# A two-block transformer kernel: normed rows transposed in token halves, routing done on both halves at once, one semaphore raised earlier

## What is computed

```python
# first block
xn = rms_norm(h, g_mix)                       # "xn" in the kernel
merged = sigmoid(gate_conv) * conv_o + sigmoid(gate_attn) * attn_o
h = h + merged @ w_out                        # the units "ax{t}{n}"
h = h + hierarchical_moe(rms_norm(h, g_ffn))  # "rn"; 4 groups of 8 experts, top 2 of one group
x = rms_norm(h, g_final)                      # "fn"
# second block
z  = modulate(rmsnorm(x), sh1, sc1)           # "zn"
hc = modulate(rmsnorm(ctx), csh1, csc1)       # "cx", gives keys and values of the context
x = x + g1 * mix(z, kv of hc)                 # ends in merged @ w_out, the units "bx{t}{n}"
x = x + g2 * peer(modulate(rmsnorm(x), sh2, sc2))   # "pn"; top 16 keys, rows fetched from tables
return rmsnorm(x, final_norm_g)
```

## Time and profile before

| what | value |
|---|---|
| median of 3 runs | 1789.43 us (1788.4 to 1790.45) |
| profiled execution, device time | 1789.33 us |
| its span on the core | 1787.5 us |
| PE busy | 1488.1 us (83%) |
| DVE busy | 856.4 us (48%) |
| ACT busy | 319.9 us (18%) |
| mean granted clock of PE | 0.914 |

### The profile page before, as it was taken

The page is one execution under the profiler, slowest core; times in us unless marked ns, Lnnn a source line. Parts: engine busy times, 40 slices in busy tenths (PEclk is TensorE's granted clock), DMA queues, the critical chain, the costliest instruction groups (busy, mean ns, idle before and its releaser), DMA issues.

```text
span 1787.5 us, 17480 instructions
## 1 busy us (share of the span) xinstructions
PE 1488.1 (83%) x6161; PEld 835.2 (47%) x6161; DVE 856.4 (48%) x1957; ACT 319.9 (18%) x632; POOL 491.9 (28%) x526
## 2 busy tenths in 40 slices
PE   6989896999999999979889999339486675849497
PEld 5866555344444434337558859314232232314143
DVE  3787125132323232235561129793847657584804
ACT  3123212110101111120330011303121111212110
POOL 1000000000000000000000004577777776777673
PEclk9999996999999999989999999769797888879699
DMA  9629572799999999974201355899999999999995
GB/s 301 249 95 336 204 274 81 318 426 428 429 428 429 428 429 428 428 275 142 94 1 59 118 212 201 307 409 409 409 409 409 409 409 409 409 410 408 406 410 214
DMA packets 135034, 565.36 MB, mean 316 GB/s; under 512 B 11350, under 2 KB 17463, under 8 KB 122493
## 3 DMA queue, kind: packets, MB, share of 16 engines
q1 hardware_dynamic: 60996, 295.88, 41.5%
q0 software_dynamic: 73968, 268.70, 38.1%
q10 hardware_dynamic: 8, 0.01, 0.0%
HBM read 563.49 MB, written 1.06 MB: 316 GB/s over the span
## 4 chain that ended last, share of the span: by engine, by line
PE 75%; DMA 10%; DVE 6%; POOL 4%; issue 3%; ACT 1%; SPq 0%; ACTq 0%; DVEq 0%; POOLq 0%
PE psum L375 52%; PE psum L952 21%; DMA ring<-in_peer_v_dram,attnT 5%; POOL ring L1113 4%; DMA ring<-in_peer_u_dram,attnT 2%; DVE scratch L2019 2%; DMA ring<-in_ada_w_dram 2%; DVE arena L1508 1%; DMA ring<-in_w_in_dram 0%; PE psum L730 0%; PE psum L736 0%; ACT actT L1150 0%; PE psum L805 0%; DVE ring L1878 0%; DVE ring L1880 0%
## 5 line engine op out<-in xcount | busy, mean ns | idle before, releaser
L952 PE MATMUL psum<-ring,arena 128*128 128x512 f32 x960 | 428.1, 609 | 215.3 <-DMA ring<-in_peer_v_dram,attnT 215.3
L1113 POOL DMA_INDIRECT ring<-in_peer_u_dram,attnT x256 | 240.2, 938 | 1189.4 <-DVE attnT L1993 1083.7
L952 PEld LDWEIGHTS psum<-ring,arena 128*128 128x128 f32 x960 | 187.4, 196 | 455.4 <-issue 321.6
L2019 DVE CUSTOM_DVE_ANT_0 scratch<-ring,psum 128x1024 f32<-128x1024 f32 x256 | 309.4, 1220 | 175.3 <-DMA ring<-in_peer_u_dram,attnT 165.2
L375 PE MATMUL psum<-ring,arena 128*64 128x512 f32 (+1 forms) x1552 | 345.2, 596 | 8.4 <-DVEq L1775 8.4
L375 PE MATMUL psum<-actT,ring 128*128 128x256 f32 (+1 forms) x1424 | 262.6, 346 | 7.0 <-DMA ring<-in_w_in_dram 4.6
L1113 POOL DMA_INDIRECT ring<-in_peer_v_dram,attnT x256 | 245.8, 960 | 79.4 <-issue 67.1
L375 PEld LDWEIGHTS psum<-actT,ring 128*128 128x128 f32 x1424 | 234.1, 194 | 34.1 <-issue 10.0
L375 PEld LDWEIGHTS psum<-ring,arena 128*64 128x64 f32 (+1 forms) x1552 | 110.7, 138 | 227.4 <-issue 205.4
L1402 ACT ACTIVATE arena<-ident,attnT 128x128 f32<-128x128 f32 x240 | 87.1, 396 | 218.6 <-PE psum L952 218.0
L1783 DVE TENSOR_TENSOR arena<-arena,psum 128x512 f32<-128x512 f32 x16 | 16.9, 1057 | 214.4 <-PE psum L375 214.4
(11 more groups left out here) (345 smaller groups left out, 1161.7 us busy)
## 6 DMA issues: line engine op xcount, KB each, us to landing
ring<-in_w_up_dram SPq DMA_DIRECT2D x32, 2048.0 KB, 15.7
ring<-in_w_down_dram SPq DMA_DIRECT2D x32, 2048.0 KB, 13.9
ring<-in_w_gate_dram SPq DMA_DIRECT2D x32, 2048.0 KB, 11.9
ring<-in_w_in_dram SPq DMA_DIRECT2D x15, 2048.0 KB, 12.9
ring<-in_ada_w_dram SPq DMA_DIRECT2D x12, 2048.0 KB, 11.5
ring<-in_w_out_dram SPq DMA_DIRECT2D x4, 2048.0 KB, 8.4
ring<-in_peer_wq_dram SPq DMA_DIRECT2D x4, 2048.0 KB, 10.5
ring<-in_w_attn_out_dram SPq DMA_DIRECT2D x2, 2048.0 KB, 8.7
```

Source lines behind the costliest of these rows:

```text
L952: last = nc.tensor.matmul(psum[:, 4 + 2 * t + n, :], diag[:, i, :], row_buf(b)[:, n * 512:(n + 1) * 512], start=first, stop=final)
L1113: pool.indirect_dma_start(out=row_buf(b), out_offset=None, in_=tab, in_offset=bass.IndirectOffsetOnAxis(ap=rowid[:, j // 4, k:k + 1], axis ...
L2019: V.tensor_tensor_reduce(dotjunk[:, i % 2, :], row_buf(b), x, 1.0, 0.0, ALU.mult, ALU.add, dots[:, t, k:k + 1]).then_inc(ev("dotted"), 1)
```

## The change

It does five things.

1. xn, rn and zn are transposed by token halves, as pn was (`half_T`, `half_out`): two banks for each half, the first emptied by ACT, the second by DVE. `tokens_T` and `pn_out` become these helpers. For xn, DVE empties its banks ahead of the rest of its parameter copies.
2. The transposes of the first half of rn and of pn stand on PE between the third and the fourth unit of the output projection. DVE norms half 0 of rn ahead of the fourth addition, and the routing matmuls of half 0 need only half 0 of `actT`.
3. The routing operations on DVE work on both halves at once where they can; the largest values and their places, which can't, are paired. The two negations (`rt_ng`, `rt_nv`) move behind `rows_out(1)`, and ACT empties `ckv0` and `ckv1` ahead of the exponentials that need them.
4. `mixed` is raised ahead of `rows_out(1)`.
5. ACT computes one square root of a constant ahead of the norm fn, after the expert loop.

```diff
+            def half_T(name, rows, ev_name, t):
+                pe.wait_ge(ev(ev_name), t + 1)
+                for n in range(2):
+                    b = bank(f"{name}{t}{n}")
+                    for c in range(4):
+                        last = nc.tensor.transpose(psum[:, b, c * P:(c + 1) * P], rows[:, t, (4 * n + c) * P:(4 * n + c + 1) * P], ident[:, :])
+                    last.then_inc(bank_full[b], 1)
...
-            out_proj(place1, "a")
-            to_T("rn", scratch, "rn_ready")
-            for g in range(4):
-                emptied(pe, f"rn{g}")
-            b = bank("route")
-            for t in range(NT):
+            pe.wait_ge(ev("amerged"), 1)
+            for t, n in ((0, 0), (0, 1), (1, 0)):
+                out_unit_rows(place1, "a", t, n)
+            half_T("rn", scratch, "rn_ready", 0)
+            out_unit_rows(place1, "a", 1, 1)
+            def route(t, b):
+                halves_out("rn", t)
...
+            half_T("rn", scratch, "rn_ready", 1)
+            b = bank("route")
+            route(0, b)
+            route(1, b).then_inc(bank_full[b], 1)
...
-            to_T("zn", scratch, "zn_ready")
-            for g in range(4):
-                emptied(pe, f"zn{g}")
+            for t in range(NT):
+                half_T("zn", scratch, "zn_ready", t)
             landed(place2, "q")
             w = pview(place2, "q")
             for t in range(NT):
+                halves_out("zn", t)
...
-            out_proj(place2, "b")
+            pe.wait_ge(ev("bmerged"), 1)
+            for t, n in ((0, 0), (0, 1), (1, 0)):
+                out_unit_rows(place2, "b", t, n)
+            half_T("pn", scratch, "pn_ready", 0)
+            out_unit_rows(place2, "b", 1, 1)
             everyday.append((4, 5, 6, 7))
...
+            a(nc.scalar.activation(stat("warm", 1), epscol[:, 0:1], ACT.Sqrt))
             squares("fn", resid, "moe_added", normjunk)
             squares("zn", resid, "x2_ready", normjunk)
-            take_T("zn", modsc[:, 0, :], mod[:, 0:KD, 0])
+            for t in range(NT):
+                half_out("zn", t, modsc[:, 0, :], mod[:, 0:KD, 0])
...
+            add_in(0, 0)
+            add_in(0, 1)
+            v(V.tensor_copy(stat("dummy", 1), epscol[:, 0:1]), "ah_ready")
+            rn_rows(0)
+            add_in(1, 0)
+            half_out("rn", 0, xgain)
+            add_in(1, 1)
+            v(V.tensor_copy(stat("dummy", 1), epscol[:, 0:1]), "ah_ready")
+            rn_rows(1)
+            half_out("rn", 1, xgain)
...
+            dve.sem_inc(ev("mixed"), 4)
             rows_out(1)
+            for t in range(NT):
+                v(V.tensor_scalar(stat("rt_ng")[:, t:t + 1], gm[:, 8 * t:8 * t + 1], -1.0, None, ALU.mult), "rt_gmax" if t else None)
+            for t in range(NT):
+                v(V.tensor_scalar(stat("rt_nv")[:, t:t + 1], em[:, 8 * t:8 * t + 1], -1.0, None, ALU.mult), "rt_top" if t else None)
             pair_rows(slotrel, 2)
...
             n_iter = dve.value_load(trips[0:1, 0:1], min_val=STEPS, max_val=MAXSTEPS)
-            dve.sem_inc(ev("mixed"), 4)
             dve.wait_ge(ev("pairx_ready"), 4)
```

More of the change, by code:

```diff
@@ L639, in merge, with out_unit_rows @@
                             last.then_inc(bank_full[b], 1)
-            def out_proj(pl, tag):
-                pe.wait_ge(ev(f"{tag}merged"), 1)
-                for t in range(NT):
[L644 to L650, removed]
+            def out_unit_rows(pl, tag, t, n):
+                landed(pl, f"wo{n}")
+                w = pview(pl, f"wo{n}")
+                b = bank(f"{tag}x{t}{n}")
+                for k in range(KD):
+                    last = mm(psum[:, b, :], mergedT[:, k, t * P:(t + 1) * P], w[:, k, :], k, KD)
+                last.then_inc(bank_full[b], 1)
             attend1()
@@ L872, in _ @@
                 last.then_inc(bank_full[b], 1)
-            out_proj(place2, "b")
-            everyday.append((4, 5, 6, 7))
[L877 to L884, removed]
+            pe.wait_ge(ev("bmerged"), 1)
[3 more added lines that the diff above has]
+            out_unit_rows(place2, "b", 1, 1)
+            everyday.append((4, 5, 6, 7))
             def tokens_back(t):
-                for n in range(2):
-                    emptied(pe, f"pn{t}{n}")
+                halves_out("pn", t)
                 for n in range(2):
@@ L914, in key_scores @@
                 last.then_inc(bank_full[b], 1)
-            tokens_T(0)
-            for n in range(2):
-                emptied(pe, f"pn0{n}")
+            halves_out("pn", 0)
             queries(0, 0)
-            tokens_T(1)
+            half_T("pn", scratch, "pn_ready", 1)
             for g in range(4):
@@ L1151, in take_T, with half_out @@
                     last(ins, f"{name}{g}")
+            def half_out(name, t, scale, bias=None):
+                ps = full(act, f"{name}{t}0")
+                for c in range(4):
+                    kw = {} if bias is None else {"bias": bias[:, c:c + 1]}
+                    ins = nc.scalar.activation(actT[:, c, t * P:(t + 1) * P], ps[:, c * P:(c + 1) * P], ACT.Identity, scale=scale[:, c:c + 1], **kw)
+                last(ins, f"{name}{t}0")
             def copy_out(name, dst, w=512, func=ACT.Copy, **kw):
@@ L1254, in _, with square @@
             squares("cx", ctxr, None, qjunk)
-            squares("rn", resid, "ah_ready")
-            take_T("rn", xgain)
+            def square(tag, src, ready, t, junk=scratch):
+                act.wait_ge(ev(ready), t + 1)
+                a(nc.scalar.activation(junk[:, t, :], src[:, t, :], ACT.Square, accum_out=stat(f"{tag}_ss")[:, t:t + 1]))
+                a(nc.scalar.activation(stat(f"{tag}_sd")[:, t:t + 1], stat(f"{tag}_ss")[:, t:t + 1], ACT.Sqrt, bias=epscol[:, 0:1], scale=1.0 / D), f"{tag}_sd")
+            square("rn", resid, "ah_ready", 0)
+            half_out("rn", 0, xgain)
+            square("rn", resid, "ah_ready", 1)
+            half_out("rn", 1, xgain)
             take_T("cx", modsc[:, 1, :], mod[:, 0:KD, 1])
+            for t in range(NT):
+                ps = full(act, f"ckv{t}")
+                nc.scalar.activation(kvt[:, t * T:t * T + P], ps[:, 0:P], ACT.Copy)
+                last(nc.scalar.activation(vtok[:, 2 + t, :], ps[:, P:2 * P], ACT.Copy), f"ckv{t}")
             act.wait_ge(ev("rt_gmax"), 1)
@@ L1341, in _ @@
                 copy_out(f"keyT{g}", keysT[:, 4 * g:4 * g + 4, :].rearrange("p c n -> p (c n)"))
-            def pn_out(t):
-                ps = full(act, f"pn{t}0")
-                for c in range(4):
-                    ins = nc.scalar.activation(actT[:, c, t * P:(t + 1) * P], ps[:, c * P:(c + 1) * P], ACT.Identity,
-                                               scale=modsc[:, 2, c:c + 1], bias=mod[:, 24 + c, 0:1])
-                last(ins, f"pn{t}0")
             def pn_square(t):
```

113 lines of the change are left out of this document (59 added, 54 removed).

## The result

The changed kernel takes 1767.97 us in the median of 4 runs (1767.25 to 1769.0), the kernel before 1789.94 us beside it. The ratio is 0.9877, interval 0.9865 to 0.9889: 22.0 us gained, where 17.2 were forecast. The time lies in the forecast range, near its lower end, so a part of the gain was not in the sum. The profiled execution takes 1767.25 us, its span 1765.4 (1787.5 before). PE is busy for 1485.8 us, 2.3 less than before, its mean granted clock is 0.919. What went is mostly waiting.

The account below looks back on a forecast made before the run. PE was taken to bound the expert loop, so gains come only where PE idles or runs slowly. 0 + 9.1 + 4.3 + 3.8 = 17.2 us off 1789.3, plus 0.1 for the median, gives 1772.2 us; range 1767.5 to 1777.5.

Parts of the forecast that it names:

- xn: At the start: evictions finish sooner but `wa` still waits for its weights; 0 gained.
- Routing: From first output projection to expert loop: loop starts at 304.7 instead of 313.85; 9.1 us gained.
- the landing of slot 1 last: Before the gate matmuls: slot 1's weights, issued at 295.95, land 8.6 us later and come last, at 304.55.
- zn: Loop to second block: table load moved into the loop's end, transposes by halves; 4.3 us gained together.
- the table load: Behind the loop: ACT's square-root table load leaves the path between first square and root; 1.28 us gained.
- pn: Behind the second output projection: idle gap closed and queries at full clock; 3.8 us gained.
- The 2.2 for the gap: Ahead of the queries: transposes before the last unit remove PE's idle time, queries start at 1061.3; 2.2 us.
- The 1.7 for the queries' clock: First 64 query records: with no gap they take 7.3 us instead of 9.01; 1.7 us.
- The weights did not land sooner: Rival at the loop's start: slot 1 lands sooner, gather last, start at 302.2; 2.4 us more, 1769.8; chance 0.10.
- The signal did what it says: Rival before the gate matmuls: raising `mixed` early doesn't release PE; routing gains 4.8, time 1776.5; chance 0.09.
- The loop is not bound by its DMAs: Rival in the expert loop: it turns DMA-bound and the kernel slower, about 1804 at 400 GB/s; chance 0.04.
- The rival on the clock: At context matmuls, q and queries: clock edges fall badly, 1776.7, or early, 1769.5; chance 0.15, both signs.

Follow-up runs that it names:

- the repetitions: The changed kernel, unaltered, run twice more on other occasions; ratios to the kernel before 0.9887 and 0.9890.
- the three runs built on it: Kernel before with one edit each: `mixed` raised early (0.9979), the added square root (0.9994), pn's first-half transposes moved (0.9981).
- The old chain: Changed kernel with the routing operations of before, half 0 then half 1 (negations stay moved); ratio to the kernel before 0.9910.
- slot 1 in two parts: Changed kernel with slot 1's first expert piece loaded as two halves, the upper issued before the wait for the context matmuls; 0.9866 to the kernel before, twice.
- cx by halves: Two-part load of slot 1 on the changed kernel, plus context norm cx by token halves, evictions on ACT; 1761.81 us, 0.9845 to the kernel before.
- the signal alone: Kernel before with only `mixed` raised ahead of `rows_out(1)` instead of just ahead of DVE's loop; ratio 0.9979.

## Why the prediction was right, and what it sized too low

**xn: right.** `wa` starts at 18.86 with its weights, the evictions are hidden. The 1.3 us lost on the way to the first projection are within what executions differ by, with the halves or without.

**Routing, 9.1 forecast, 10.6 measured (10.6 and 10.4 in the repetitions).** The mechanism holds: logits sooner (2.0 us, 1.4 forecast), DVE's 22 records in 3.8 us (4.4 forecast), the signal no longer last, the landing of slot 1 last at 8.5 us (8.6 forecast). The context matmuls start 0.6 us sooner than forecast and take 8.83 us instead of the 9.74 of before: 1.5 in all, the whole error. The start: the sum had the counting matmuls last and took them at 2.16 us, as before; they took 1.30. ACT's emptying of cx came last, by 1.49 us, and it was 0.5 us ahead of its forecast, as the transposes of cx were. The duration is PE's clock. In the kernel before, and in the three runs built on it, the granted clock stayed at 0.50 through the counting matmuls (0.64 us for the first two records) and for 5 us or more of the context matmuls. In all ten profiles with the halves of rn it rose by the end of the cx transposes or under the counting matmuls. The old chain shows that the wait behind them counts too: there the clock was at 1.00 and fell again in the 3.64 us ahead of the counting matmuls. That the counting matmuls were not the last to release the context matmuls cost the sum nothing, but ACT was the next thing to take away.

**zn, 4.3 forecast, 4.6 measured.** 1.2 for the table load (1.28), 3.4 for the halves (3.0). The extra is again the transposes, 3.30 us instead of the 3.94 that the sum took. What the sum left out is q behind them, 1.9 us over all profiles (2.2 in this pair), of which 1.5 reach the second projection.

**pn, 3.8 forecast, 4.2 measured, one reason partly wrong.** The 2.2 for the gap is 2.5 and repeats. The 1.7 for the queries' clock came out to the digit, but by luck: it was taken from the one profile with the dip. "The gap had cost PE its full clock" holds for that profile alone (granted clock 0.50 at 1065 and 1066 us); the same gap cost 1.7 us there and 0.07 in two others.

**The rivals.** The weights did not land sooner, at a full piece (8.4 to 8.6 us each time). The signal did what it says. The loop is not bound by its DMAs: its turns take 29.16 us before and after, PE is busy for 451.8 of the 452.0 us from 318 to 770 us in both, and with slot 1 in two parts it starts 2.8 us sooner and q comes 4.3 us sooner, both counted from the first projection. The rival on the clock saw the places and read them as chance of both signs. Shorter waits moved it one way, at the context matmuls and at q. At the first gate matmuls the change gained nothing of the kind (15.32 before, 15.60 after), only the loads in two parts did. The Trainium skill ("TensorE: Matmul & The Clock Gate", section "What's actually happening") says that the moment of the change moves from run to run. The traces agree, with 20.88 to 22.04 us for q in one and the same order, but with 3.4 us of idle time ahead, as before, it is 22.57 to 23.71: the spread sits on a mean that differs between the two.

**Between executions.** Of the 22.1 us between the spans, the three forecast stages hold 19.4 and q 2.2. The rest is -1.3 at the start, -0.3 in the loop and +2.0 at the end; over all profiles the start shows no difference, and at the end 0.7 repeated. The two later ratios, 0.9887 and 0.9890, put the gain at 20 us.

## What to carry to other kernels

When a wait is taken away, look up which event comes next and cost only the distance to it; here the same line was worth 4.2 us or 6.3, by what stood behind it. When PE idles ahead of dense matmuls, look up the granted clock behind the wait and add what the lower level costs there, and read both from several profiles before a duration goes into a sum. A piece that waits for a slot of which only half is in use can be loaded in two parts, and here evictions ordered by what the next matmul needs first (6.11 us of ACT) beat those with less work in all (4.18).

## What the runs showed of the hardware

The first 64 gate records take 13.95 us where PE waits 1.40 us ahead of them, three times out of three. After 3.96 to 4.17 us of waiting they take 15.40 to 15.65 us five times and 16.9 twice, and after 8.4 to 11.0 us 15.3 to 15.4 us four times. The granted clock over them is 1.00 in the first group, 0.82 where they take 16.9, and 0.89 to 0.91 otherwise. A longer wait costs no more here: what counted was whether the clock had fallen. So the piece that landed late cost its wait and 1.5 us behind it.

A short wait is not free everywhere. Ahead of the context matmuls PE waits 1.35 to 1.53 us in eight profiles, with 1.3 us of counting matmuls and another wait of some 0.5 us before that. There the clock fell to 0.50 each time, in the changed kernel between 287 and 291 us, and the 32 records took 8.68 to 8.83 us. Without the wait (cx by halves) it did not fall, and they took 7.15:

```profile
283.00:290.10 7.10, 7.10 (x34) 5.97 (x33) 5.93 (x31) 2.48 (x8) 0.00 (x0) 1.00 0.00 1
```

On one chip the stage behind the key scores took 820 to 821 us, on the others 712 to 714, with every stage ahead of it alike. In a stretch of 500 us there, first the kernel before, then that with the signal alone on the slow chip:

```profile
1200.00:1700.00 500.00, 344.69 (x772) 150.70 (x771) 323.57 (x761) 92.89 (x222) 366.98 (x389) 0.85 1.03 409
```

```profile
1200.00:1700.00 500.00, 320.03 (x670) 135.49 (x670) 300.22 (x716) 68.09 (x185) 311.18 (x330) 0.80 0.91 347
```

The row fetches there moved 347 GB/s instead of 409 (347 to 350 in all four profiles on that chip). The cause was not tried; it is a reason to time versions side by side.
